# Two-block transformer layer: value projection in token rows ahead of the heads, SSM projection and seven gates inside them

## The reference, cut to what matters

```python
xn = rmsnorm(h, norm1_gain)
q, k, v, u, gates = jnp.split(xn @ w_in, splits, axis=-1)
q = rope(rmsnorm(q, q_norm_gain), cos, sin)      # 8 heads x 2 x 64
k = rope(rmsnorm(k, k_norm_gain), cos, sin)
a = softmax(q0 @ k0.T) - lam * softmax(q1 @ k1.T)   # causal
o = rmsnorm(a @ v, subln_gain)                   # v: 8 heads x 128
attn_branch = o @ w_attn_proj
s = s5_layer(u, ...)                             # state space scan, gelu, GLU with w_glu
ssm_branch = s @ w_ssm_proj
g_attn, g_ssm = jnp.split(sigmoid(gates), 2, axis=-1)
h = h + (g_attn * attn_branch + g_ssm * ssm_branch) @ w_out
```

## Time and profile before

| | |
|---|---|
| median of 3 runs | 1394.95 us (1394.46 to 1395.45) |
| the profiled execution | 1394.86 us, its span 1393.1 us |
| TensorE busy | 1373.4 us, 99% |
| VectorE, ScalarE busy | 686.0 us, 833.5 us |
| mean granted TensorE clock | 0.997 of full |
| loop of heads | 177 to 386 us of the span |

### The profile page before, as it was taken

One profiled execution on the slowest core, in us unless ns is written; L12 is line 12 of the kernel. 1 busy time (PEld: TensorE's weight loads), 2 busy tenths in 40 slices (PEclk: granted clock), 3 DMA queues, 4 the chain that ended last, 5 costly groups with the idle time before them and its releaser, 6 DMA issues.

```text
span 1393.1 us, 18371 instructions
## 1 busy us (share of the span) xinstructions
PE 1373.4 (99%) x6666; PEld 1114.7 (80%) x6666; DVE 686.0 (49%) x1317; ACT 833.5 (60%) x1215; POOL 204.9 (15%) x240
## 2 busy tenths in 40 slices
PE   7999999999999999999999999999999999999998
PEld 4888877777788888888888887777798888888887
DVE  6993478888643455554145154745255301213324
ACT  7556667778665656665356366765667654535443
POOL 1111110100011111111111111100111111111112
PEclk9999999999999999999999999999999999999999
DMA  9996976665679888898988887754678797887973
GB/s 300 216 181 174 227 171 149 143 161 137 136 200 221 193 185 194 189 205 181 213 181 190 190 195 181 153 144 117 150 168 195 179 209 183 197 198 181 211 165 91
DMA packets 82598, 252.67 MB, mean 181 GB/s; under 512 B 16720, under 2 KB 19920, under 8 KB 82512
## 3 DMA queue, kind: packets, MB, share of 16 engines
q0 software_dynamic: 32400, 116.93, 46.7%
q1 hardware_dynamic: 48272, 131.06, 31.2%
q10 hardware_dynamic: 1840, 3.54, 0.7%
HBM read 126.98 MB, written 3.41 MB: 94 GB/s over the span
## 4 chain that ended last, share of the span: by engine, by line
PE 94%; DVE 3%; ACT 1%; DMA 1%; issue 0%; SPq 0%; DVEq 0%; ACTq 0%
PE pg L614 28%; PE pg L616 27%; PE pg L615 27%; PE ps L786 2%; PE py L862 1%; PE ps L1044 1%; PE ps L794 1%; PE ps L1052 1%; DMA act_lo<-w_raw 1%; PE py L1062 1%; DMA hid<-x 0%; DVE acc L1755 0%; DVE acc L1752 0%; DVE rstd L1752 0%; DVE pairs L1752 0%
## 5 line engine op out<-in xcount | busy, mean ns | idle before, releaser
L614 PE MATMUL pg<-x_hi,w_hi 128*128 128x512 f32 x1072 | 422.8, 394 | 0.0
L616 PE MATMUL pg<-x_hi,w_lo 128*128 128x512 f32 x1072 | 417.6, 390 | 0.0
L615 PE MATMUL pg<-x_lo,w_hi 128*128 128x512 f32 x1072 | 417.4, 389 | 0.0
L572 POOL DMA_DIRECT2D w_lo<-w_raw x221 | 190.4, 862 | 1146.6 <-ACT w_lo L1175 1071.7
L1174 ACT ACTIVATE w_hi<-w_raw 128x1024 fp32r<-128x1024 f32 (+1 forms) x215 | 224.3, 1043 | 103.1 <-PE pg L616 101.2
L614 PEld LDWEIGHTS pg<-x_hi,w_hi 128*128 128x128 f32 x1072 | 201.3, 188 | 53.2 <-issue 12.1
L616 PEld LDWEIGHTS pg<-x_hi,w_lo 128*128 128x128 f32 x1072 | 201.2, 188 | 42.4
L615 PEld LDWEIGHTS pg<-x_lo,w_hi 128*128 128x128 f32 x1072 | 201.4, 188 | 41.6 <-issue 1.0
L1175 ACT ACTIVATE w_lo<-w_raw 128x1024 fp32r<-128x1024 f32 (+1 forms) x215 | 223.2, 1038 | 0.0
L614 PE MATMUL pg<-act_hi,w_hi 128*128 128x512 f32 x424 | 165.1, 389 | 0.0
L615 PE MATMUL pg<-act_lo,w_hi 128*128 128x512 f32 x424 | 165.0, 389 | 0.0
(11 more groups left out here) (437 smaller groups left out, 1824.2 us busy)
## 6 DMA issues: line engine op xcount, KB each, us to landing
w_raw<-weights SPq DMA_DIRECT2D x218, 512.0 KB, 4.7
w_lo<-w_raw POOLq DMA_DIRECT2D x213, 512.0 KB, 5.6
kq_rot<-kq_raw SPq DMA_DIRECT2D x64, 64.0 KB, 2.0
w_raw<-weights SPq DMA_DIRECT2D x8, 384.0 KB, 3.5
w_lo<-w_raw POOLq DMA_DIRECT2D x8, 384.0 KB, 4.2
hid<-x SPq DMA_DIRECT2D x4, 512.0 KB, 5.5
hid<-x ACTq DMA_DIRECT2D x8, 256.0 KB, 5.6
act_lo<-w_raw POOLq DMA_DIRECT2D x4, 512.0 KB, 7.3
```

Source lines behind the costliest of these rows:

```text
L572: pool.dma_start(low_of(u)[:, 0:n], w_raw[:, s, 0:n], accum_op=ALU.add).then_inc(lo_in[s], 16)
L614: pe.matmul(bank[:], wh, xh(k), start=n == 0, stop=False)
L615: pe.matmul(bank[:], wh, xl(k), start=False, stop=False)
L616: last = pe.matmul(bank[:], wl, xh(k), start=False, stop=n == len(ks) - 1)
```

## The change

- The value of four heads is made at once: `values(group)` takes four units and keeps a 128-token block of the input as the stationary side (x_hi, x_lo); the weights of the four heads stream as 512 columns. The result has tokens on partitions, as the later products need it. It fills all four banks of `ps`, each with 8 slices from four pieces, 6 products per bank and piece. The transposes, `v_raw`, and the copy out of `px` are gone.
- Each of the four weight pieces holds two slices for four heads, so its load gathers runs of 1 KB.
- `values(0)` stands after nine gates, ahead of the SSM chunk outputs, `values(1)` after q of head 0; the two GLU units follow it.
- The place of v in passes 1 to 7 goes to the four SSM units (passes 1 to 4) and to three gates (5 to 7). Seven gates now get their sigmoid late.
- Some buffers move: g_lo and s_lo into hid, s_hi into gates and rstd, the values of heads 0 to 3 into gates 1 to 4, pr, tri and the sq_lo tiles elsewhere. `in_pg` counts the tiles that really go through `pg`.

```diff
-GATES_FIRST, GATES_LAST = (8, 9, 10, 11, 12, 13, 14, 15, 0, 1, 2, 3), (4, 5, 6, 7)
+GATES_FIRST, GATES_LAST = (8, 9, 10, 11, 12, 13, 14, 15, 0), (1, 2, 3, 4, 5, 6, 7)
+GROUP = HEADS // 2
+def filler(h):
+    return ("ssm", h - 1) if h <= 4 else ("gate", GATES_LAST[h - 5])
...
-    u += [("k", 0), ("v", 0), ("glu", 0), ("glu", 1), ("q", 0)] + [("ssm", n) for n in range(4)]
+    u += [("v", h) for h in range(GROUP)] + [("k", 0), ("q", 0)] + [("v", GROUP + h) for h in range(GROUP)]
+    u += [("glu", 0), ("glu", 1)]
     for h in range(1, HEADS):
-        u += [("k", h), ("q", h), ("v", h)]
-    u += [("gate", g) for g in GATES_LAST]
+        u += [("k", h), ("q", h), filler(h)]
+    u += [("gate", g) for g in GATES_LAST[HEADS - 5:]]
...
+                        group = weights[UNIT[("v", h)]:UNIT[("v", h)] + GROUP, :, 2 * P * piece:2 * P * piece + 2 * P]
+                        sp.dma_start(w_raw[:, u % RING].rearrange("p (h k) m -> p h (k m)", k=2),
+                                     group.rearrange("h p c -> p h c")).then_inc(w_landed[u % RING], 16)
...
+            def values(group):
+                banks = []
+                for p in range(GROUP):
+                    u = UNIT[("v", GROUP * group + p)]
+                    s = u % RING
+                    pe.wait_ge(lo_in[s], lows(u))
+                    wh, wl = (a[:, s].rearrange("p (h k) m -> p h k m", k=2) for a in (w_hi, w_lo))
+                    for i in range(QB):
+                        if p == 0 and i % 2 == 0:
+                            bank = s_use((("v", group), i // 2))
...
+                        for k in range(2):
+                            xh, xl = (x[:, 2 * p + k, P * i:P * i + P] for x in (x_hi, x_lo))
+                            pe.matmul(banks[i], xh, wh[:, :, k], start=p == 0 and k == 0, stop=False)
+                            pe.matmul(banks[i], xl, wh[:, :, k], start=False, stop=False)
+                            last = pe.matmul(banks[i], xh, wl[:, :, k], start=False, stop=p == GROUP - 1 and k == 1)
...
+            values(0)
+            chunk_outputs(0)
+            chunk_outputs(1)
             named(("k", 0), XH, XL)
-            named(("v", 0), XH, XL)
+            output_turns(0)
+            output_turns(1)
+            named(("q", 0), XH, XL)
+            pe.wait_ge(blocks_made, 1)
+            kq_sums(0, "k", 0)
+            values(1)
+            kq_sums(0, "q", 1)
             for m in range(SSM_T):
                 glu(m)
-            named(("q", 0), XH, XL)
-            for n in range(4):
-                ssm(n)
...
                 if attends:
-                    x_use(("vt", g))
-                    evacuated(pe, ("v", g))
-                    for j in range(QB):
-                        last = pe.transpose(px[:, P * j:P * j + P], v_raw[:, P * j:P * j + P], ident)
-                    last.then_inc(px_full, 1)
                     scores(g, 0)
                     scores(g, 1)
...
                 if h < HEADS:
-                    named(("v", h), XH, XL)
+                    if h <= 4:
+                        ssm(h - 1)
+                    else:
+                        named(filler(h), XH, XL)
                     kq_sums(h, "q", 1)
...
                 if h < HEADS:
                     rope_step(h, "k", 0, rs_k, kk)
+                if h <= 4:
+                    ssm_out(2 * h - 2)
                 if attends:
                     combine(g, 2)
                     combine(g, 3)
+                if h <= 4:
+                    ssm_out(2 * h - 1)
                 if h < HEADS:
                     rope_step(h, "q", 1, rs_q, qq)
```

More of the change, by code:

```diff
@@ L130, with in_pg @@
     TILES_AFTER.append(_o)
+def in_pg(name):
+    o = TILE[name]
+    return o - sum(GROUP for h in (0, GROUP) if TILE[("v", h)] < o)
 SPLIT = {}
@@ L447, in ps_ready @@
         def ps_ready(eng, name):
-            eng.wait_ge(ps_full, SUSE[name] + 1)
+            uncounted = sum(SUSE[(("v", group), 1)] < SUSE[name] for group in range(2))
+            eng.wait_ge(ps_full, SUSE[name] + 1 - uncounted)
             return ps[SUSE[name] % 2]
@@ L857, in _ @@
                     y_use(("pv", h - 2))
-                    px_read(pe, ("vt", h - 2))
+                    for half in range(2):
+                        ps_read(pe, (("v", (h - 2) // GROUP), half))
                     ps_read(pe, ("t", h - 2, 2))
@@ L1324, in _, with values_out @@
[L1324 to L1329 removed]
+            def values_out(group):
+                for i in range(QB):
+                    use = (("v", group), i // 2)
+                    if i == 0:
+                        ps_ready(act, use)
+                    if i == 2:
+                        act.wait_ge(tile_done, TILE[("v", GROUP * group + GROUP - 1)] + 1)
+                    ins = act.activation(vv[group][:, i], ps[SUSE[use] % 2][:, i % 2], ACT.Copy)
+                    if i % 2 == 1:
+                        ins.then_inc(ps_free[SUSE[use] % 2], 1)
@@ L1379, in late_gate @@
                 free(act.activation(gates[:, g], done(("gate", g)), ACT.Copy), ("gate", g))
+            for h in range(GROUP):
+                ahead(("v", h))
+            values_out(0)
             ahead(("k", 0))
+            outputs_out(0)
+            outputs_out(1)
             kq_out(0, "k", 0, "kg")
-            ahead(("v", 0))
-            free(act.activation(v_raw[:], done(("v", 0)), ACT.Copy), ("v", 0))
+            act.dma_start(rtab[:], rope).then_inc(r_landed, 16)
+            turned_out(0)
+            turned_out(1)
+            ahead(("q", 0))
+            ps_read(act, ("yt", 0))
+            ps_read(act, ("yt", 1))
+            for t in range(SSM_T):
+                put(act.activation(g_hi[:, t], y5[:, t], ACT.Copy), xhi_done)
+            ln_and_exp()
+            kq_out(0, "q", 1, "qg")
+            ahead(("v", GROUP))
+            head_root(("ssq_k", 0), 0, C_EPS, 1.0 / 64, rs_k)
+            for h in range(GROUP + 1, HEADS):
+                ahead(("v", h))
+            values_out(1)
+            head_root(("ssq_q", 0), 1, C_EPS64, 1.0, rs_q)
             for m in range(SSM_T):
@@ L1428, in _ @@
                 if h <= HEADS:
-                    ahead(("q", h) if h < HEADS else ("gate", 5))
+                    ahead(("q", h) if h < HEADS else ("gate", GATES_LAST[4]))
                 if attends:
@@ L1447, in _ @@
                 if h < HEADS:
-                    ahead(("v", h))
-                    free(act.activation(v_raw[:], done(("v", h)), ACT.Copy), ("v", h))
+                    ahead(filler(h))
+                    if h > 4:
+                        late_gate(GATES_LAST[h - 5])
                     head_root(("ssq_q", h), 1, C_EPS64, 1.0, rs_q)
```

177 lines of the change are left out of this document (86 added, 91 removed).

## The result

The changed kernel takes 1398.78 us (median of 9 runs, 1397.26 to 1399.11), the kernel before 1394.99 beside it: ratio 1.0024, 95% interval 1.0015 to 1.0033. A second set of 11 against 33 runs gave 1398.57 and 1395.19: 1.0022 (1.0012 to 1.0031); one of these 11 took 3560.8 us, in the slow state, and is left out of the ratio. So the change makes the kernel slower by 3.4 to 3.8 us. The forecast was 1397.9.

The account below looks back on a forecast made before the run. TensorE, busy 1373.4 of 1393.1 us, was taken as the bound, with waits between its instructions. Terms -0.5 - 0.3 + 2.84 + 0.7 + 0.2 = +2.94 us gave 1397.9 (own ends 1396.9 and 1399.1; range with rivals 1394.8 to 1402).

Parts of the forecast that it names:

- Transposes: Removing 32 value transposes: heads 2 to 8 gain nothing, hidden in a wait for VectorE's copy; first head gains; -0.5 us.
- Token rows: 192 value products reading four runs of 128 columns, with bank changes every 6 products: taken as 0, at most +7.7 us.
- SSM products: Two SSM products on VectorE in each of heads 1 to 4 delay the copy pt and second scores: +2.84 us.
- 4 x 0.71: Scores of heads 2 to 5 each start 0.71 us later behind VectorE's delayed copy: +2.84 us.
- in the 0.71: Next key unit starts 0.27 us late for its bank, counted inside the 0.71 us delay per head, not on top.
- First SSM wait: Before the heads, moving the SSM products away removes a wait at their first product: -0.3 us.
- GLU wait: Before the heads, the third GLU half unit waits for the bank ScalarE's sigmoid frees: +0.7 us (0.4 to 1.0).
- Value weights: Value weight loads in 1 KB runs push the second value unit's low part, landing just in time: +0.2 us (0 to 0.5).
- rival of late value weights: Fourth value unit's weights land 5 us later between toep pieces; TensorE waits, say, 3 us: 1401 us; chance 0.12.
- transposes that pay in every head: Removed transposes gain 0.44 us in each head, -3.5 us in all, and SSM products fit idle time: 1392.0; chance 0.07.
- the strided one: Strided operand or bank changes in the value products cost from 3 up to 7.7 us: 1401 to 1405.6; chance 0.11.
- VectorE absorbs: VectorE's 0.76 us idle time and 1 us of waits in each head take in the SSM products: 1395.0; chance 0.10.

Follow-up runs that it names:

- ssm_act: Against the changed kernel, ScalarE copies the SSM tiles out of PSUM in passes 1 to 4 and VectorE multiplies them next pass; 1395.91 us, ratio 0.9998.

## Why the prediction was right, and where it wasn't

**Transposes (-0.5 us): right.** The kernel with only them left out gained 0.42 us, all ahead of the first pass's end, and the later periods stayed at 24.70. In the changed kernel the gate passes have 24.69, not 24.26. The argument from the copy into the same bank held: the second pair of scores starts 1.78 us behind the seven transposes with and without the four.

**Token rows (0 us, bound 7.7): right.** Both groups of 96 products run at 0.227 us each. The runs of 128 columns and the bank change every 6 products cost nothing. The rule of the Trainium skill (SBUF — State Buffer, Door 1: The DMA port swizzle), by which such runs pay nothing, agrees with the trace.

**SSM products (+2.84 us): right in mechanism, one of four terms mis-sized.** Measured 3.35: 0.70, 0.75 and 0.73 in three passes, where 0.71 was predicted, and 1.17 at the crossing from pass 1 to pass 2. The step that failed is "4 x 0.71", which gave the first crossing the 0.76 us of idle time read in pass 4. There the kernel before had only 0.31:

```profile
203.49 0.69 DVE L1752 TENSOR_TENSOR qq<-rope_a,kq_rs 128x512 f32<-128x512 f32 x1
204.49 0.69 DVE L2060 COPY pt<-ps 128x512 f32<-128x512 f32 x1 [0.31 <-PE ps L794]
```

The prediction's own formula, 1.44 - 0.31 + 0.03, gives 1.16 there, and 1.17 was measured. The row was in the trace; I took the steady pass for the first. Within a steady pass the bank wait of the key unit was priced at 0.27 and called "in the 0.71". It was 0.37 and 0.08 more: the key unit started 0.14 us behind the end of the product that frees its bank (248.46 to 248.60), not 0.06. It did lie inside, since the whole came to 0.73. But it is a cost of its own as well, and stays when the second product is moved away.

**First SSM wait (-0.3 us): right.** The first SSM product now stands in pass 1 behind the scores, where a value unit began before. It starts 1.70 us after them and runs 0.50 us, as that unit's first product did, so nothing is added there, and the gap ahead of 154.00 is gone from the order.

**GLU wait (+0.7 us): right.** The gap is 0.90 against 0.23, and 0.07 more at the product behind it. With the sigmoid ahead of the weight pair the gap is gone.

**Value weights (+0.2 us, 0 to 0.5): wrong in cause, and the size stays open.** The wait at the second value unit was 0 to 1.6 us in the executions seen, 0.6 more on average than with the old units, but three traces against seven don't show that the change adds it. Not the 1 KB pieces make the wait, but the Toeplitz loads issued ahead. The term was read from one execution's row, which is at the low end of what the same kernel shows. The rival of late value weights named another unit, the fourth; no trace showed a wait there.

The sum of what was measured, -0.4 - 0.3 + 3.35 + 0.7 + 0.6, is +3.9 us; the medians differ by 3.4 to 3.8. The forecast's +2.9 lacks 0.5 from the first crossing and, if the 0.6 belongs to the change, 0.4 from the weights. The two profiled executions, 2.4 us apart, close without the weights: -0.6 at the start (the third group of input products at 30.5 instead of 31.1), 0.0 from there to pass 1, +0.7 over pass 1 and the first crossing, +2.1 over the other periods, and +0.2 behind. The ends of its own range, 1396.9 and 1399.1, are narrower than its terms give (1396.6 and 1399.3), and the measured median lies inside either. Of the rivals, the one with transposes that pay in every head and the strided one are excluded. "VectorE absorbs" was wrong for this place of the products, but right about the idle time: there is room for them at the start of the next pass, once ScalarE has freed the bank (ssm_act).

## What to carry to other kernels

Adding work to an engine with spare time costs what lies between its place and the next thing that others wait for: 1.4 us on an engine busy for 22 of 25 us cost 0.7 to 1.2 in one place and nothing in another. Price such a term at each place where it falls, the first and the last round of a loop apart from the steady ones. Work removed from behind a wait for another engine pays only when the wait's own chain starts earlier: 32 transposes paid 0.4 us, moving seven by three products paid 0.69 per pass.

## What the runs showed of the hardware

- A product of 128x512 right behind a wait runs 0.47 to 0.50 in place of 0.39 us, and the next starts 0.30 to 0.34 later instead of 0.23. Each wait costs 0.07 to 0.11 on top of itself.
- One 512 KB write took 6.8 us or 10.8 to 14.0 us, by what eight loads of short rows did beside it; behind four of these a 512 KB load took 19.0 us, where medians of 9.9 to 12.1 had been usual for the weight loads of the stretch (the two profiles of the changed kernel). Moving the traffic moved the delay to another transfer.
- Single executions of one kernel differ by 1 to 4 us. In the traces it comes from three places: that transfer, the start, and the stretch behind the heads. From the first probability-value product of the last pass to the end of the span that stretch takes 1014.8 to 1016.4 us in the fourteen traces; what in it varies was not looked into. At the start TensorE, busy for 4.2 and 5.0 of the 8 us before, ran from 16 to 22 us at a granted clock of 0.50 (1.2 GHz) throughout in the kernel before, and at 0.72 on average, so partly at the 2.4 GHz level, in the second look at the changed one. The third group of input products starts between 30.5 and 31.2 us in the traces. The clock is not the whole of it: the second look at the kernel before was granted 0.72 in the same window too, but its first input product starts at 17.3 instead of 16.7, and the third group at 31.1 as in its first look. The windows of the kernel before (first look) and the changed one (second look), columns as in the earlier trace rows, then that first input product:

```profile
16.00:22.00 6.00, 5.26 (x13) 4.12 (x14) 5.72 (x9) 6.00 (x9) 1.88 (x2) 0.50 1.06 330
```

```profile
16.00:22.00 6.00, 5.32 (x16) 4.28 (x17) 5.72 (x9) 6.00 (x9) 1.88 (x2) 0.72 1.05 329
```

```profile
17.28 0.47 PE L630 MATMUL pg<-x_hi,w_hi 128*128 128x512 f32 x1 [2.82 <-DVE x_lo L1752]
```
